# Latent attention scores: one f32 product, or three products of high and low parts fetched per head

## The reference, cut to what matters

```python
qm = (rms_norm(cq, mla_q_norm_w[i]) @ mla_w_uq[i]).reshape(b, s, 8, 96)
q_nope, q_pe = qm[..., :64], apply_rope(qm[..., 64:], positions, 32)
kv = (rms_norm(ckv, mla_kv_norm_w[i]) @ mla_w_ukv[i]).reshape(b, s, 8, 128)
k_nope, v_m = kv[..., :64], kv[..., 64:]
k_pe = apply_rope(krope[:, :, None, :], positions, 32)      # one for all heads
q_full = concat([q_nope, q_pe]); k_full = concat([k_nope, broadcast(k_pe)])
mo = causal_attention(q_full, k_full, v_m, 96 ** -0.5)       # softmax over masked q k^T
```

## Time and profile before

| | |
|---|---|
| Median of the runs | 1949.79 us |
| The profiled execution | 1949.6 us |
| Its span in the profile | 1947.7 us |
| TensorE busy | 1937.9 us, 99% |
| VectorE, ScalarE, GpSimd busy | 1060.3, 931.6, 1069.1 us |
| Moved by DMA | 221.55 MB, mean 114 GB/s |
| Granted TensorE clock, mean | 0.999 |

### The profile page before, as it was taken

How to read it: one execution, slowest core, us unless ns; L and a number is a source line. 1 busy time by engine, 2 the same in 40 slices (tenths; PEclk the granted TensorE clock), 3 DMA queues, 4 the chain that set the end, 5 groups by cost and what they waited for, 6 DMA issues and landing times.

```text
span 1947.7 us, 28650 instructions
## 1 busy us (share of the span) xinstructions
PE 1937.9 (99%) x9242; PEld 1624.2 (83%) x9242; DVE 1060.3 (54%) x1926; ACT 931.6 (48%) x1643; POOL 1069.1 (55%) x1418
## 2 busy tenths in 40 slices
PE   9999999999999999999999999999999999999998
PEld 8888888888888888888888888888888888888887
DVE  6565888887655333321144668888875543333111
ACT  6444767767434222233344456766674442222332
POOL 6654453454655555557755645445446555555674
PEclk9999999999999999999999999999999999999999
DMA  6443332334532322233344333233355322222232
GB/s 234 123 123 97 104 103 92 93 108 141 195 131 92 103 97 97 97 111 97 105 141 138 109 108 101 89 103 98 103 174 173 124 98 97 97 95 93 82 90 94
DMA packets 161140, 221.55 MB, mean 114 GB/s; under 512 B 54930, under 2 KB 73106, under 8 KB 160532
## 3 DMA queue, kind: packets, MB, share of 16 engines
q1 hardware_dynamic: 136752, 183.81, 29.6%
q10 hardware_dynamic: 24292, 36.49, 5.4%
HBM read 197.96 MB, written 22.29 MB: 113 GB/s over the span
## 4 chain that ended last, share of the span: by engine, by line
PE 98%; DMA 1%; ACT 0%; POOL 0%; DVE 0%; issue 0%; SPq 0%; DVEq 0%; ACTq 0%
PE proj L637 24%; PE proj L639 24%; PE proj L638 24%; PE score L637 2%; PE score L638 2%; PE score L639 2%; PE flip L703 2%; PE score L685 2%; PE score L855 1%; PE score L857 1%; PE score L689 1%; PE score L688 1%; PE att L618 1%; PE att L619 1%; PE att L617 1%; PE score L869 1%
## 5 line engine op out<-in xcount | busy, mean ns | idle before, releaser
L594 POOL TENSOR_TENSOR w_lo<-raw,w_hi 128x256 fp32r<-128x256 f32 x1372 | 1064.0, 808 | 858.0 <-ACT w_hi L1189 857.6
L637 PE MATMUL proj<-h_hi,w_hi 128*128 128x512 f32 x1552 | 612.8, 395 | 0.0
L639 PE MATMUL proj<-h_hi,w_lo 128*128 128x512 f32 x1552 | 605.2, 390 | 0.0
L638 PE MATMUL proj<-h_lo,w_hi 128*128 128x512 f32 x1552 | 604.1, 389 | 0.0
L1189 ACT ACTIVATE w_hi<-raw 128x1024 fp32r<-128x1024 f32 x344 | 362.5, 1056 | 192.8 <-PE proj L639 55.0
L639 PEld LDWEIGHTS proj<-h_hi,w_lo 128*128 128x128 f32 x1552 | 291.3, 188 | 62.0
L637 PEld LDWEIGHTS proj<-h_hi,w_hi 128*128 128x128 f32 x1552 | 291.6, 188 | 57.7 <-issue 0.6
L638 PEld LDWEIGHTS proj<-h_lo,w_hi 128*128 128x128 f32 x1552 | 291.7, 188 | 57.5
L637 PE MATMUL proj<-hid_hi,w_hi 128*128 128x512 f32 x330 | 129.0, 391 | 0.0
L639 PE MATMUL proj<-hid_hi,w_lo 128*128 128x512 f32 x330 | 128.5, 389 | 0.0
L638 PE MATMUL proj<-hid_lo,w_hi 128*128 128x512 f32 x330 | 128.4, 389 | 0.0
(11 more groups left out here) (433 smaller groups left out, 3178.8 us busy)
## 6 DMA issues: line engine op xcount, KB each, us to landing
raw<-in_w_in SPq DMA_DIRECT2D x224, 256.0 KB, 2.9
raw<-in_w_gate_up SPq DMA_DIRECT2D x176, 256.0 KB, 2.8
raw<-in_w_down SPq DMA_DIRECT2D x96, 192.0 KB, 2.4
gate_in<-gate_scratch ACTq DMA_DIRECT2D x48, 256.0 KB, 4.3
gate_scratch<-gate_out ACTq DMA_DIRECT2D x44, 256.0 KB, 2.0
raw<-in_w_mem_kv SPq DMA_DIRECT2D x32, 256.0 KB, 2.9
raw<-in_w_o_diff SPq DMA_DIRECT2D x32, 256.0 KB, 2.8
raw<-in_w_out SPq DMA_DIRECT2D x32, 256.0 KB, 2.8
```

The lines of the kernel that those rows point to most:

```text
L594: ins = g.tensor_tensor(w_lo[s][:, cols], raw[s % 2][:, cols], w_hi[s][:, cols].bitcast(F32), ALU.subtract)
L637: mm(o, hi[:, c:c + width], rh, start=start and k == 0, stop=False)
L638: mm(o, hi[:, c:c + width], rl, start=False, stop=False)
L639: ins = mm(o, lo[:, c:c + width], rh, start=False, stop=stop and k == n - 1)
```

## The change

The queries, the rotated query rows and the keys are split once per layer into high and low parts side by side (`[P, 2, SEQ]`, 512 KB a tile). Ten tiles per layer (four query, two rotated, four key) go to three new DRAM tensors. Per head three DMAs fetch 256, 128 and 256 KB into `mq` and `mk`; the rotated key rows are put into `mk` once per layer. The score is three products of float32r parts.

SyncE gets all new transfers, at these places: `store_queries` behind slot (Z, 8); `store_keys` between slots (B 0, 1) and (B 0, 2); `load_latent` for head 0 before slot (B 0, 3), for head 1 at the end of step 0, and for head h+1 in steps h = 1 to 6 between `load_values` and slot (h, 2).

```diff
@@ SyncE
+            def store_queries(l):
+                for t in range(4):
+                    if t == 3:
+                        for r in range(2):
+                            sp.wait_ge(ur_split.sem, ur_split.at(l, "Z", 0, r + 1))
+                            sp.dma_start(r_latent[r, :, :, :], r_parts[r][:, :, :].bitcast(F32)).then_inc(q_stored.sem, 16)
+                    sp.wait_ge(uq_split.sem, uq_split.at(l, "Z", 0, t + 1))
+                    sp.dma_start(q_latent[t, :, :, :], q_parts[t][:, :, :].bitcast(F32)).then_inc(q_stored.sem, 16)
+
+            def store_keys(l):
+                for t in range(4):
+                    sp.wait_ge(k_nope_split.sem, k_nope_split.at(l, "Z", 0, t + 1))
+                    sp.dma_start(k_latent[t, :, :, :], k_parts[t][:, :, :].bitcast(F32)).then_inc(k_stored.sem, 16)
+
+            def load_latent(l, h):
+                if h == 0:
+                    sp.wait_ge(q_stored.sem, q_stored.at(l, "Z", 0, 96))
+                    sp.wait_ge(k_stored.sem, k_stored.at(l, "Z", 0, 64))
+                else:
+                    sp.wait_ge(score_full.sem, score_full.at(l, "B", h - 1, 3))
+                sp.dma_start(mq[0:NOPE, :, :].bitcast(F32), q_latent[h // 2, half_of(h), :, :]).then_inc(latent_loaded.sem, 16)
+                sp.dma_start(mq[NOPE:NOPE + ROPE_M, :, :].bitcast(F32), r_latent[h // 4, rope_of(h), :, :]).then_inc(latent_loaded.sem, 16)
+                sp.dma_start(mk[0:NOPE, :, :].bitcast(F32), k_latent[h // 2, half_of(h), :, :]).then_inc(latent_loaded.sem, 16)
@@ SyncE, stages Z and B
                 slot(l, "Z", 0, 8, *whole(w_in, l, T_DV))
+                store_queries(l)
                 for h in range(HEADS - 1):
                     slot(l, "B", h, 0, *whole(w_in, l, T_DV + (h + 1)))
...
                     slot(l, "B", h, 1, *whole(w_in, l, T_DQ + (h + 1)))
                     if h:
                         load_values(l, h)
+                        load_latent(l, h + 1)
+                    else:
+                        store_keys(l)
                     slot(l, "B", h, 2, *gate(l, GATES_B + 2 * h))
+                    if h == 0:
+                        load_latent(l, 0)
                     slot(l, "B", h, 3, *whole(w_in, l, T_DK + (h + 1)))
                     slot(l, "B", h, 4, *gate(l, GATES_B + 2 * h + 1))
                     if h == 0:
                         store_values(l, 0)
+                        load_latent(l, 1)
@@ TensorE
-                            ins = mm(o, mqT[0:96, cols], mkT[0:96, 0:(t + 1) * P], start=t != 0, stop=t == group[-1])
+                            q, q_lo, k, k_lo = mq[0:96, 0, cols], mq[0:96, 1, cols], mk[0:96, 0, 0:(t + 1) * P], mk[0:96, 1, 0:(t + 1) * P]
+                            mm(o, q, k, start=t != 0, stop=False)
+                            mm(o, q, k_lo, start=False, stop=False)
+                            ins = mm(o, q_lo, k, start=False, stop=t == group[-1])
...
-                    pe.wait_ge(uq_copied.sem, uq_copied.at(l, "Z", 0, n + 1))
+                    pe.wait_ge(uq_split.sem, uq_split.at(l, "Z", 0, n + 1))
...
-                    pe.wait_ge(k_nope_copied.sem, k_nope_copied.at(l, "Z", 0, t + 1))
+                    pe.wait_ge(k_nope_split.sem, k_nope_split.at(l, "Z", 0, t + 1))
...
             def latent_scores(l, h):
-                pe.wait_ge(mla_ready.sem, mla_ready.at(l, "B", h, 1))
-                pe.wait_ge(mq_copied.sem, mq_copied.at(l, "B", h, 1))
+                pe.wait_ge(latent_loaded.sem, latent_loaded.at(l, "B", h, 48))
                 causal_scores(l, h, 0)
@@ ScalarE
-                copy(gate_in[:, k, :], b[:, :]).then_inc(uq_copied.sem, 1)
+                copy(q_parts[k][:, 0, :], b[:, :]).then_inc(uq_copied.sem, 1)
...
-                copy(k_nope[:, k, :], b[:, :]).then_inc(k_nope_copied.sem, 1)
+                copy(k_parts[k][:, 0, :], b[:, :]).then_inc(k_nope_copied.sem, 1)
...
+            def query_turned(l, r):
+
+                act.wait_ge(mla_ready.sem, mla_ready.at(l, "Z", 0, r + 1))
+                copy(r_parts[r][:, 0, :], r_whole[r][:, :]).then_inc(ur_copied.sem, 1)
...
-                query_rows(l, n)
@@ VectorE
+            def query_nope_low(l, t, b):
+
+                ve.wait_ge(uq_copied.sem, uq_copied.at(l, "Z", 0, t + 1))
+                v.tensor_tensor(q_parts[t][:, 1, :], b[:, :], q_parts[t][:, 0, :].bitcast(F32), ALU.subtract).then_inc(uq_split.sem, 1)
...
+            def key_turned(l):
...
+                chain(rope(k_turned, score[0], rows, cos_m, sin_m, SHUF_M, (qk_split, qk_split.at(l, "B", 0, 1))))
+                chain(v.tensor_copy(mk[rows, 0, :], k_turned[rows, :]))
+                v.tensor_tensor(mk[rows, 1, :], k_turned[rows, :], mk[rows, 0, :].bitcast(F32), ALU.subtract).then_inc(mla_ready.sem, 1)
...
-                latent_rows(l, n)
@@ VectorE, stage Z
+                for t in range(3):
+                    query_nope_low(l, t, latent_bank[t])
+                for r in range(2):
+                    query_turned_low(l, r)
+                query_nope_low(l, 3, latent_bank[3])
+                key_turned(l)
...
-                latent_rows(l, 0)
+                for t, b in enumerate(latent_bank):
+                    key_nope_low(l, t, b)
```

More of the change, by code:

```diff
@@ L93, in build_trunk @@
 def build_trunk(nc, x, mem, x_rows, positions, w_in, w_ckv, diff_lambda, w_o_diff, mla_w_uq, mla_w_ukv, w_o_mla, w_mem_kv,
-                w_o_cross, w_out, w_gate_up, w_down, gain_cols, out, table_scratch, x_scratch, gate_scratch, rstd_scratch, v_scratch, c_scratch):
+                w_o_cross, w_out, w_gate_up, w_down, gain_cols, out, table_scratch, x_scratch, gate_scratch, rstd_scratch, v_scratch, c_scratch, q_latent, r_latent, k_latent):
     ctx = ExitStack()
@@ L140, in build_trunk @@
         rstd = here("rstd", [P, SEQ])
+        gate_in_at = cursor[0]
         gate_in = here("gate_in", [P, 6, SEQ])
@@ L188, in build_trunk @@
         v_lo = at("v_lo", T + 22 * KB, [P, NT, P], F32R)
-        k_nope = at("k_nope", T + 24 * KB, [P, HEADS // 2, SEQ])
+        mq = at("mq_hi_lo", T + 24 * KB, [P, 2, SEQ], F32R)
+        mk = at("mk_hi_lo", T + 28 * KB, [P, 2, SEQ], F32R)
         qT = at("qT", T + 28 * KB, [P, SEQ])
         kT = at("kT", T + 30 * KB, [P, SEQ])
-        mqT = at("mqT", T + 32 * KB, [P, SEQ])
-        mkT = at("mkT", T + 34 * KB, [P, SEQ])
+        q_parts = [at(f"q_parts{t}", (16 * KB, 20 * KB, T + 32 * KB)[t], [P, 2, SEQ], F32R) for t in range(3)]
+        q_parts.append(nc.alloc_sbuf_tensor_at("q_parts3", [P, 2, SEQ], F32R, offset=gate_in_at))
+        k_parts = [at(f"k_parts{t}", (32 + 4 * t) * KB, [P, 2, SEQ], F32R) for t in range(4)]
+        r_parts = [nc.alloc_sbuf_tensor_at(f"r_parts{r}", [P, 2, SEQ], F32R, offset=gate_in_at + (4 + 4 * r) * KB) for r in range(2)]
+        r_whole = [nc.alloc_sbuf_tensor_at(f"r_whole{r}", [P, SEQ], F32, offset=gate_in_at + (6 + 4 * r) * KB) for r in range(2)]
+        k_turned = at("k_turned", T + 38 * KB, [P, SEQ])
         vT = at("vT", T + 36 * KB, [P, SEQ])
@@ L262, in build_trunk @@
         uq_copied = Tally(sem("uq_copied"), "act", Z=(4, 1))
+        uq_split = Tally(sem("uq_split"), "ve", Z=(4, 1))
+        ur_copied = Tally(sem("ur_copied"), "act", Z=(2, 1))
+        ur_split = Tally(sem("ur_split"), "ve", Z=(2, 1))
         k_nope_copied = Tally(sem("k_nope_copied"), "act", Z=(4, 1))
+        k_nope_split = Tally(sem("k_nope_split"), "ve", Z=(4, 1))
+        q_stored = Tally(sem("q_stored"), "act", Z=(96, 1))
+        k_stored = Tally(sem("k_stored"), "act", Z=(64, 1))
+        latent_loaded = Tally(sem("latent_loaded"), "act", B=(48, HEADS))
         mv_high = Tally(sem("mv_high"), "act", Z=(4, 1))
         mv_split = Tally(sem("mv_split"), "ve", Z=(4, 1))
-        mq_copied = Tally(sem("mq_copied"), "act", B=(1, HEADS))
         low_copied = Tally(sem("low_copied"), "act", B=(1, HEADS))
@@ L299, in build_trunk @@
         gate_scaled = Tally(sem("gate_scaled"), "ve", E=(12, 2))
-        mla_ready = Tally(sem("mla_ready"), "ve", Z=(3, 1), B=(1, HEADS))
+        mla_ready = Tally(sem("mla_ready"), "ve", Z=(3, 1))
         diff_ready = Tally(sem("diff_ready"), "ve", B=(2, HEADS))
@@ L369, in build_trunk @@
         y_scaled = [sem("y_scaled0"), sem("y_scaled1")]
-        vec_step = Tally(sem("vec_step"), "ve", N1=(4, 1), C=(2, CROSS), A=(1, 1), P=(14, 1), B=(13, HEADS - 1), L=(7, 1),
+        vec_step = Tally(sem("vec_step"), "ve", N1=(4, 1), C=(2, CROSS), A=(1, 1), P=(16, 1), B=(13, HEADS - 1), L=(7, 1),
                          E=(4, 2), N2=(4, 1), G=(2, FT // 2))
         tallies = [
-            sq_done, sq_added, sum_high, sum_split, slot_hi, slot_done, tile_done, uq_copied, k_nope_copied, mv_high, mv_split, mq_copied, low_copied, om_done, score_full, bias_ready,
```

(44 more changed lines are left out.)

## The result

The changed kernel takes 2084.66 us (2083.86 to 2085.36) against 1949.80 before: a ratio of 1.0692, 95% interval 1.068 to 1.0705. It is 134.9 us slower. The forecast was 2064 (2034 to 2096).

A forecast was written before the change was run, and what follows sets the result against it. TensorE's own instruction time was taken to bound the kernel (busy 1937.9 of 1947.7 us). Twelve stalls of 9.9 us (119), less 4.2 from the cheaper product, gave +115 on 1949.6: 2064 us, range 2034 to 2096.

The forecast's parts named there:

- the band of the forecast: Whole kernel: twelve TensorE stalls, each followed by half clock, giving 2050 to 2080 us; chance 50%.
- the rival with late stores and a full queue: Slots landing at 9.7 instead of 7.4 us after score start (28 us), or head 0 late (8 us): 2085 to 2105, 16%.
- The product: Latent scores on TensorE: 1.90 us instead of 2.16 per head, gaining 0.26, 16 times, 4.2 us.
- The upper bound of 6.5 us: Most that the cheaper latent-score product could gain: 0.4 us per head, if the next unit's late start falls away.
- The wait in the load queue: SyncE waits for latent scores before slot (h, 2), steps 1 to 6, both layers, holding ScalarE and TensorE's attend: 12 stalls.
- S: Start time of a head's latent scores on TensorE; head 4's, at 330.30 us, served as the forecast's example.
- The size of one stall: TensorE idle before attend: 7.7 us (6.9 to 10); 8.7 with later waits at full clock, 9.9 with half clock.
- a free landing and a burst of three: Slot landing 3.1 us after issue with nothing ahead, against 4.4 to 7.0 us each for three 256 KB DMAs in a row.
- The estimate from the Trainium skill: Held slot's landing from 2.0 us fixed plus bytes over 436 GB/s, giving a stall of 7.1 us; not used in the sum.
- The clock: TensorE falls to half speed after every stall, up to 5.5 us; 2.2 us extra taken, bounds 0 and 2.8.
- The waits I named at full clock: Behind the delayed attend: 0.8 us for the gate copy, 0.2 for the latent scores' maxima and exponentials; 1 us per stall.
- The stage before the heads: Added VectorE subtractions and SyncE stores cost 0; head 0's operands land near 179 against 181.33; up to 4 us per layer.

The follow-up runs named there:

- experiment 1: Changed kernel with the latent loads of steps 1 to 6 moved one place down, behind slot (h, 2): 1946.90 us, ratio 0.9985 to the kernel before.
- experiment 3: Changed kernel with latent loads behind slot (h, 2) and the score again one f32 product of the high parts: 1951.19 us, ratio 1.0007.
- experiment 4: Kernel before plus only SyncE's wait for the latent scores ahead of slot (h, 2), steps 1 to 6, no transfers: 2049.35 us, ratio 1.0508.
- experiment 7: Changed kernel, load queue untouched, ScalarE making slot (h+1, 2)'s high part only behind the next head's exponentials: 1962.20 us, ratio 1.0065.
- experiment 6: Changed kernel, same waits and latent DMAs, but from head 2 on each fetches only 4 rows: 2058.46 us, ratio 1.0561.
- experiment 8: Changed kernel with 36 extra 512-column TensorE products between latent scores and attend in steps 0 to 5: 2074.59 us, ratio 1.0642.

## Why the prediction was right

The time lies in the range, 20.7 us above the forecast; both the direction and the mechanism hold. It lies above the band of the forecast (2050 to 2080, 50%) and at the lower end of the rival with late stores and a full queue (2085 to 2105, 16%). Of that rival the landing came out in part; the stores did not. By the steps:

- **The product.** Forecast 0.26 per head, read from the attend product of the same widths. Measured 0.24 in the timeline, 0.27 by experiments 1 and 3. Right. (The upper bound of 6.5 us doesn't follow from the rows: with twelve products in 1.85 us instead of 2.16 the gain is 0.31 per head, 5.0 in all.)
- **The wait in the load queue.** Right in place, count and direction: 12 stalls, started by SyncE's wait in its steps 1 to 6 and handed on by ScalarE's program order to TensorE, which is then in its steps 0 to 5. Experiments 1, 4 and 7 show each link by itself: without the place, without the transfers, without the order. (By the rows the wait ends about 7 us after ScalarE wants the slot, at S + 2.05 against 325.24, not 5; no sum used that number.)
- **The size of one stall.** This is where the 20 us are. The wake (S + 2.1) was right. The high part was forecast at S + 7.4, with 9.7 as the far end; in the mean of the twelve it started at S + 9.3. Three terms were too small. The slot's second DMA went out at S + 4.2, not 3.8, since a latent DMA takes 0.56 us to issue and not 0.43. With nothing ahead of it, it lands not 3.1 but about 3.5 us later (experiment 4). And the 0.5 us for the 640 KB ahead is 1.6 (experiment 6, in the mean). They make 0.4 + 0.4 + 1.1 = 1.9 us; the copies behind them took 0.1 less than forecast. Of the two rows I had, a free landing and a burst of three, I leaned to the wrong one: transfers issued within 1.7 us of each other behaved as a burst. Over all stalls it is 9.44 us against the 7.7 of the forecast: 12 x 1.74 = 21 us. The estimate from the Trainium skill (DMA: Bandwidth & Descriptors, Anatomy of one DMA), 7.1 us of stall, was further off; the section gives its figures for one DMA issued by GpSimd, and here five stand in SyncE's queue. The measurement decides.
- **The clock.** It fell in every stall, as forecast from the kernel's end. I put 2.2 us for it, in place of the waits behind, and 2.2 is the mean of the twelve. That the two agree so closely is luck: the forecast came to it from 2.8 us lost and a part hidden, and 2.2 lost is what was measured. The net price of the clock was forecast at 1.2 us per stall (9.9 less 8.7) and is 0.8 to 1.0 by experiment 8. The waits I named at full clock, 0.8 for the gate copy and 0.2 for the softmax chain, are 0.3 and 0.4 there. The Trainium skill (TensorE: Matmul & The Clock Gate, What's actually happening) has the low clock as the default that activity releases; the rows of the stall agree, with 0.50 at the resumed work and 1.00 some 3.5 us on.
- **The stage before the heads.** No wait there in the changed kernel, as forecast, but with little to spare. I had head 0's operands landed near 179. The last of them was issued at 175.81 and took 5.3 us to land, so 181.1, and the scores start at 181.65. In experiment 1 TensorE did wait 0.3 us for it. The landing was put too early here for the same reason as in the stalls, and it cost nothing by half a microsecond.
- So the miss of 20.7 us is the length of the idle stretch.

## What to carry to other kernels

A queue that issues loads in order is an engine like the others. Before putting a wait into it, ask what stands behind it there, which engine is the first to want that load, and what that engine has behind it in turn: here one line in the wrong place turned a gain of 3.5 us into a loss of 135, from SyncE through ScalarE and VectorE to TensorE. A new transfer that must wait for late work belongs behind the loads that are wanted earlier.

Where a stop on TensorE like those here (5.7 to 9.8 us) is forecast, add the half clock after it, but look for waits that the slower stretch hides; and price a load behind others by a burst row, not by a free one. When one stall out of twelve is shown in detail, take the mean of all before multiplying by twelve: here the stall shown was the longest.

## What was not expected of the hardware

- 640 KB put 1.6 us on the landing of the slot behind them in the mean (1.0 to 2.2, stall by stall), although they are issued over 1.7 us. Their whole transfer at the 347 GB/s of the earlier trace rows would take 1.9 us, so the issuing time hid little of it.
- The time to issue a DMA on SyncE fell with the rows, but not in proportion: 0.27 to 0.30 us for 4 rows of 4 KB (experiment 6), 0.48 for 64 rows, and 0.58 for the 32 rotated rows. Why the smaller of the two full ones takes longer is open.
- The way back to full clock took 2.9 to 6.2 us of work, differently in each of twelve like stalls, 4.4 in the mean; the slow products at the kernel's start had lasted 5.5, under a clock shown as 1.00.
